# Two transformer blocks on one core: seven block products in place of eight for the feed-forward up projections

## The reference, cut to what matters

```python
D_MODEL, SEQ, D_FF = 1024, 512, 2816

def _swiglu(h, w13, w2):
    g, u = jnp.split(h @ w13, 2, axis=-1)
    return (jax.nn.silu(g) * u) @ w2

def _sublayer(x, fn, pre_g, post_g, shift, scale, gate, res_w):
    h = _rmsnorm(x, pre_g) * (1.0 + scale[:, None, :]) + shift[:, None, :]
    y = _rmsnorm(fn(h), post_g)
    return x + res_w * (1.0 + gate[:, None, :]) * y
...
        mod = (c_act @ ada_w[l] + ada_b[l]).reshape(bsz, N_SUB, 3, D_MODEL)
```

## Time and profile before

| | us |
|---|---|
| median of 3 runs | 3217.52 |
| lowest and highest | 3217.0, 3223.48 |
| span of the profiled execution | 3213.7 |

### The profile page before, as it was taken

How to read it: one execution, slowest core, us unless ns; L and a number is a source line. 1 busy time by engine, 2 the same in 40 slices (tenths; PEclk the granted TensorE clock), 3 DMA queues, 4 the chain that set the end, 5 groups by cost and what they waited for, 6 DMA issues and landing times. The chain is left out here.

```text
span 3213.7 us, 52487 instructions
## 1 busy us (share of the span) xinstructions
PE 3045.3 (95%) x20065; PEld 2461.7 (77%) x20065; DVE 1728.6 (54%) x3224; ACT 1155.9 (36%) x2075; POOL 1349.1 (42%) x893
## 2 busy tenths in 40 slices
PE   5999999899999999999999999999888889999998
PEld 4888876678887888877788887987666667778887
DVE  6445478654445566232666114537677754674443
ACT  3222235432223322234332223226544434435343
POOL 3444443244444434453434444224767660143332
PEclk8999999999999999999999999999999999999999
DMA  7655432155544554332255334213222233222222
GB/s 216 195 184 173 158 85 73 53 170 183 183 156 153 167 180 135 97 90 79 86 163 151 94 93 136 79 53 112 65 58 58 56 107 73 91 77 71 82 66 59
DMA packets 641381, 366.02 MB, mean 114 GB/s; under 512 B 107902, under 2 KB 634132, under 8 KB 640688
## 3 DMA queue, kind: packets, MB, share of 16 engines
q1 hardware_dynamic: 633216, 351.57, 37.2%
q10 hardware_dynamic: 6640, 10.49, 1.1%
q0 software_dynamic: 1344, 1.44, 0.2%
HBM read 334.27 MB, written 24.97 MB: 112 GB/s over the span
## 5 line engine op out<-in xcount | busy, mean ns | idle before, releaser
L270 POOL TENSOR_TENSOR w_lo<-w_raw,w_hi 128x1024 fp32r<-128x1024 f32 (+1 forms) x333 | 786.6, 2362 | 1316.6 <-ACT w_hi L262 1263.9
L335 PE MATMUL acc<-h,w_hi 128*128 128x512 f32 x2256 | 704.4, 393 | 0.0
L262 ACT ACTIVATE w_hi<-w_raw 128x1024 fp32r<-128x1024 f32 (+1 forms) x332 | 344.6, 1038 | 941.1 <-PE acc L335 687.9
L335 PEld LDWEIGHTS acc<-h,w_hi 128*128 128x128 f32 x2256 | 417.3, 188 | 84.6 <-issue 1.8
L335 PE MATMUL acc<-h,w_lo 128*128 128x512 f32 x1128 | 440.3, 390 | 0.0
L335 PE MATMUL acc<-hid,w_hi 128*128 128x512 f32 x1056 | 326.3, 390 | 0.0
L716 DVE SCALAR_TENSOR_TENSOR ada_part<-ada_raw,c_act,ada_part 128x256 f32<-128x256 f32 x672 | 315.0, 489 | 18.6
L335 PEld LDWEIGHTS acc<-h,w_lo 128*128 128x128 f32 x1128 | 211.7, 188 | 45.8
L335 PEld LDWEIGHTS acc<-hid,w_hi 128*128 128x128 f32 x1056 | 197.3, 188 | 40.7
L335 PE MATMUL spare<-h,w_hi 128*128 128x512 f32 x688 | 211.7, 389 | 0.0
L335 PE MATMUL acc<-hid,w_lo 128*128 128x512 f32 x528 | 205.6, 389 | 0.0
(11 more groups left out here) (700 smaller groups left out, 6094.7 us busy)
## 6 DMA issues: line engine op xcount, KB each, us to landing
w_raw<-in_ffn_w SPq DMA_DIRECT2D x240, 512.0 KB, 4.0
ada_raw<-in_ada_w SPq DMA_DIRECT2D x88, 1024.0 KB, 5.0
w_raw<-in_od_w_in SPq DMA_DIRECT2D x32, 512.0 KB, 4.0
w_raw<-in_ffn_w SPq DMA_DIRECT2D x32, 384.0 KB, 3.1
w_raw<-in_ev_w_in SPq DMA_DIRECT2D x22, 512.0 KB, 3.9
image<-inverse_wait SPq DMA_DIRECT2D x144, 64.0 KB, 2.1
first_ada<-in_ada_w SPq DMA_DIRECT2D x8, 1024.0 KB, 12.4
w_raw<-in_ab_w_in SPq DMA_DIRECT2D x16, 512.0 KB, 4.0
```

Source lines behind the costliest of these rows:

```text
L262: act.activation(K.w_hi[:, first % SPLIT, 0:tiles, :], K.raw[:, first % RAW, 0:tiles, :], ACT.Copy).then_inc(K.hi_ready, 1)
L270: pool.tensor_tensor(K.w_lo[:, first % SPLIT, 0:tiles, :], K.raw[:, first % RAW, 0:tiles, :], K.w_hi[:, first % SPLIT, 0:tiles, :].bitcast ...
L335: mm = pe.matmul(out, w[:, slot, k, :], moving(ap, k, tokens), start=first and k == 0 and p == 0, stop=last and k == tiles - 1 and p == le ...
```

## The change

With Strassen's scheme (in Winograd's form) a product of 2 by 2 blocks takes seven block products in place of eight, and some additions of blocks. The blocks here are halves of the 1024 features (4 tiles each), the two chunks of a turn (gate and up), and halves of the 512 tokens (256 columns each). So:

- Turns 0 to 2 of each phase stay as they are (without modulation pieces). Turns 3 to 21 are made of seven products of 4 tiles by 3 passes with 256 columns: 84 in place of 48 products of TensorE.
- Four sums of blocks of `h` are made once a phase, on VectorE, then split: high part on ScalarE, low part on VectorE (128 by 1024 elements each). For them the entry keeps the full `h` too (`h_full`): ScalarE writes each block twice, and `low` reads the full block and the high part, both from SBUF.
- Per turn VectorE makes four sums of weights: one operation of 1024 elements and two of 512, all from SBUF to SBUF. GpSimd makes the low parts in five pieces, two of 1024 and three of 512 elements (2 of 1024 before); ScalarE the high parts likewise.
- The seven results in PSUM are combined by VectorE in four operations a turn (three of 512 elements and one of 256), with one copy of 256 on ScalarE; silu now reads SBUF.
- The high and low parts of the hidden values are no longer made in each turn but all at the end: 22 high parts on ScalarE, 17 low parts on VectorE, 5 on GpSimd, while the first down turn runs.
- Pieces of modulation are spread anew: one vector's eight sums a turn at most, in three portions between the other operations. Phases 0 and 2 have one a turn in turns 3 to 21, and 7 and 8 in down turns; phase 3 has one in turns 3 to 13, the two vectors of four pieces in turns 14 to 21, and 8 pieces of two vectors in its down turns; phase 5 four pieces in turns 3 to 10 and 8 in its down turns.

The core of the diff (blank lines left out):

```diff
+        if full is not None:
+            act.activation(full[:, b, :], S.tp[b % 2][:], ACT.Identity, bias=shift[:, b:b + 1]).then_inc(S.h_full, 1)
...
+        if full is not None:
+            dve.wait_ge(S.h_full, b + 1)
+            dve.tensor_tensor(S.h[:, LO, b, :], full[:, b, :], S.h[:, HI, b, :].bitcast(F32), ALU.subtract).then_inc(S.h_ready, 1)
+            return
...
+PLAIN = 3
+HALF = SEQ // 2
+KH = DB // 2
+HI_PLACE = {1: 1, 7: 2, 6: 3, 3: 4, 4: 5}
+LO_PLACE = {5: 1, 7: 1, 1: 2, 2: 2, 6: 3, 3: 4, 4: 5}
+ADA_UP = {0: {t: (t - 3, None) for t in range(3, FB)},
+          2: {t: (t + 23, None) for t in range(3, FB)},
+          3: {**{t: (t + 50, None) for t in range(3, 14)}, **{t: (64 + (t - 14) // 2, t % 2) for t in range(14, FB)}},
+          5: {t: (76 + (t - 3) // 2, (t - 3) % 2) for t in range(3, 11)}}
+ADA_DOWN = {0: range(19, 26), 2: range(45, 53), 3: range(68, 76), 5: range(80, 88)}
...
+        moving = {1: h[:, :, 0:KH, 0:HALF], 2: h[:, :, KH:DB, 0:HALF], 3: h[:, :, KH:DB, HALF:SEQ],
+                  5: t_of[0], 6: t_of[1], 7: t_of[2], 4: t_of[3]}
...
+                for t in range(PLAIN + 2, FB):
+                    n = base + 2 * t
+                    sp.wait_ge(S.lo, 5 * (t - PLAIN - 1))
+                    chunk_load(n + 1, up.sources[1](t))
+                    sp.wait_ge(S.left_done, t - PLAIN - 1)
+                    chunk_load(n, up.sources[0](t))
+                    ada_until(t)
...
+                def lo(t, p):
+                    tau = t - PLAIN
+                    pool.wait_ge(S.hi, 5 * tau + HI_PLACE[p])
+                    if p == 7:
+                        pool.wait_ge(S.sums, 3 * tau + 2)
+                    elif p in (1, 6):
+                        pool.wait_ge(S.sums, 3 * tau + 3)
+                    if p in (1, 7):
+                        out, full, top = both_lo(t, p), both_full(t, p), both_hi(t, p)
+                    else:
+                        out, full, top = lo_of(t, p), full_of(t, p), hi_of(t, p)
+                    pool.tensor_tensor(out, full, top.bitcast(F32), ALU.subtract).then_inc(S.lo, 1)
...
+                for j in range(2):
+                    split_lo(pool, K, up, 2, 2, j, 8)
+                for t in turns:
+                    for p in (7, 1, 6, 3, 4):
+                        lo(t, p)
+                pool.sem_inc(K.lo_ready, 2 * count)
+                for j in range(2):
+                    split_lo(pool, K, down, 0, 0, j, tiles[j])
+                for j in range(8, 13):
+                    pool.wait_ge(S.hid_hi, j + 1)
+                    pool.tensor_tensor(hid[:, j, :], hid_full[:, j, :], hid_hi(j).bitcast(F32),
+                                       ALU.subtract).then_inc(S.hid_pool, 1)
...
+                quick_pre_act(act, K, S, base, shift, update, full=h_full)
+                plain(0)
+                for j in range(2):
+                    split_hi(act, K, up, 2, 2, j, 8)
+                hi(PLAIN, 1)
+                term_hi(1, 2)
+                hi(PLAIN, 7)
+                hi(PLAIN, 6)
+                plain(1)
+                term_hi(2, 3)
+                term_hi(0, 3)
+                hi(PLAIN, 3)
+                hi(PLAIN, 4)
+                term_hi(3, 4)
+                plain(2)
+                for t in turns:
+                    if t + 1 < FB:
+                        hi(t + 1, 1)
+                    else:
+                        act.sem_inc(K.hi_ready, 2 * count)
+                        down_hi(0)
+                    copy_first(t)
+                    if t > PLAIN:
+                        silu(t - 1)
+                    if t + 1 < FB:
+                        for p in (7, 6, 3, 4):
+                            hi(t + 1, p)
+                    else:
+                        down_hi(1)
+                hidden_hi(0, 16)
+                silu(FB - 1)
+                split_hi(act, K, down, 0, 0, 2, tiles[2])
+                hidden_hi(16, FB)
...
+                def product(t, p):
+                    pe.wait_ge(S.lo, 5 * (t - PLAIN) + LO_PLACE[p])
+                    for k in range(KH):
+                        for part in (HI, LO):
+                            pe.matmul(out_of[p], hi_of(t, p)[:, k, :], moving[p][:, part, k, :], start=k == 0 and part == HI, stop=False)
+                    for k in range(KH):
+                        mm = pe.matmul(out_of[p], lo_of(t, p)[:, k, :], moving[p][:, HI, k, :], start=False, stop=k == KH - 1)
+                    if p in done:
+                        mm.then_inc(done[p], 1)
...
+                    if tau == 0:
+                        pe.wait_ge(S.prod_ready, 2)
+                        pe.wait_ge(S.h_full, DB)
+                        pe.wait_ge(S.t_ready, 4)
+                    else:
+                        pe.wait_ge(S.left, tau)
+                    product(t, 1)
+                    product(t, 2)
+                    if pending is not None:
+                        ada_pe(pe, K, FIRST_ADA + pending, K.ada_of(pending)[0].vecs, K.ada_acc, S.ada_cols)
+                    q, v = ADA_UP[index].get(t, (None, None))
+                    pending = None if v == 0 else q
+                    product(t, 6)
+                    if tau:
+                        pe.wait_ge(S.u_second, tau)
+                    product(t, 5)
+                    product(t, 7)
+                    if tau:
+                        pe.wait_ge(S.outer, tau)
+                    product(t, 3)
+                    product(t, 4)
...
+                def sums_first(t):
+                    tau = t - PLAIN
+                    slots_free(dve, t)
+                    chunk_landed(dve, t, 0)
+                    chunk_landed(dve, t, 1)
+                    q = (base + 2 * t) % RAW
+                    quarters = K.raw[:, q:q + 2].rearrange("p c (a k) w -> p (c a) (k w)", a=2)
+                    both = (K.w_sums[:, 0].rearrange("p (a k) c -> p a (k c)", a=2), K.z[:, 4:6, :])[t % 2]
+                    dve.tensor_tensor(both, quarters[:, 2:3].broadcast_to([P, 2, KH * P]), quarters[:, 0:4:3],
+                                      ALU.subtract).then_inc(S.sums, 1)
+                    dve.wait_ge(S.sums, 3 * tau + 1)
+                    dve.tensor_tensor(sum_full(t, 6), full_of(t, 1), sum_full(t, 5),
+                                      ALU.subtract).then_inc(S.sums, 1)
+                def sums_second(t):
+                    tau = t - PLAIN
+                    dve.wait_ge(S.sums, 3 * tau + 2)
+                    dve.tensor_tensor(sum_full(t, 3), full_of(t, 2), sum_full(t, 6),
+                                      ALU.subtract).then_inc(S.sums, 1)
+                def combine_left(t):
+                    tau = t - PLAIN
+                    dve.wait_ge(S.left_done, tau + 1)
+                    dve.wait_ge(S.copied, tau + 1)
+                    if tau:
+                        dve.wait_ge(S.sil, tau)
+                    dve.tensor_tensor(left, pairs[0], p1_copy.broadcast_to([P, 2, HALF]), ALU.add).then_inc(S.left, 1)
+                def combine_right(t):
+                    tau = t - PLAIN
+                    dve.wait_ge(S.right_done, tau + 1)
+                    dve.wait_ge(S.left, tau + 1)
+                    dve.tensor_tensor(right, pairs[1], left[:, 1:2].broadcast_to([P, 2, HALF]), ALU.add).then_inc(S.right, 1)
+                    dve.wait_ge(S.right, tau + 1)
+                    dve.tensor_tensor(u_rows[:, 1], right[:, 1], out_of[5], ALU.add).then_inc(S.u_second, 1)
+                def combine_outer(t):
+                    dve.wait_ge(S.turn_done, t - PLAIN + 1)
+                    dve.wait_ge(S.u_second, t - PLAIN + 1)
+                    dve.tensor_tensor(right, right, pairs[2], ALU.add).then_inc(S.outer, 1)
+                def gated(t):
+                    dve.wait_ge(S.sil, t - PLAIN + 1)
+                    row = hid_full[:, t, :].rearrange("p (a c) -> p a c", a=2)
+                    dve.tensor_tensor(row, row, u_rows, ALU.mult).then_inc(S.prod_ready, 1)
...
+                quick_pre_dve(dve, K, S, shift, update, h_full)
+                dve.wait_ge(S.h_full, DB)
+                b11, b12 = h_full[:, 0:KH, 0:HALF], h_full[:, 0:KH, HALF:SEQ]
+                b21, b22 = h_full[:, KH:DB, 0:HALF], h_full[:, KH:DB, HALF:SEQ]
+                whole = [t[:, LO] for t in t_full]
+                term(1, whole[0], b12, b11, ALU.subtract)
+                term(2, whole[1], b22, whole[0], ALU.add)
+                plain(0)
+                sums_first(PLAIN)
+                sums_second(PLAIN)
+                term(3, whole[2], b12, b22, ALU.add)
+                term(4, whole[3], b21, whole[1], ALU.subtract)
+                term_lo(1, 1)
+                plain(1)
+                term_lo(2, 2)
+                term_lo(0, 3)
+                term_lo(3, 4)
+                plain(2)
+                pending = None
+                for t in turns:
+                    q, v = ADA_UP[index].get(t, (None, None))
+                    vec = v or 0
```

(28 more changed lines are left out.)

369 lines of the change are left out of this document (255 added, 114 removed).

## The result

| | before | after |
|---|---|---|
| median, us | 3217.3 (3217.0 to 3223.5) | 3357.3 (3353.0 to 3357.9) |
| span of the profiled execution | 3213.7 | 3350.7 |

A forecast was written before the change was run, and what follows sets the result against it. The prediction took TensorE, busy 95% of the span, as the bound, and port waits as the new turns' bound. Its terms, -50 - 4 + 17 + 21 + 21 + 5 + 21 = +31 us on 3217.5, gave 3249; range 3205 to 3285.

The forecast's parts named there:

- Products: Strassen turns on TensorE: 256-column products at 0.1198 us, 10.53 us a turn with a piece, saving 0.8 in each of 76.
- The port: SBUF port shared by VectorE and GpSimd: waits make a loop of 11.05 us a turn, longer than TensorE's 10.53.
- So they take turns: VectorE's SBUF sums and GpSimd's splits alternate at the port; two GpSimd operations lose 0.43 us each.
- Turns 3 to 21: Strassen turns in four phases: five at 10.5 us, then 14 at 11.05; 878 us become 828, -50.
- Entry: Entry blocks: the low part waits for GpSimd's addition, 0.95 us later for each of six blocks in three phases; +21 us.
- Start of turn 3: Before turn 3: port work outlasts TensorE's cover by about 5.3 us; +21 for four phases, +5 for the clock.
- End: First down turn: low parts alternate between VectorE and GpSimd, 1.72 us a pair; 5.7 us, 4 in phase 5; +21.
- Pieces in down turns: Modulation pieces moved into down turns lengthen those by 0.93 us each, with a last piece in the first; +17 us.
- Their sums hide beside 15 us of products: Down turns: VectorE's sums for the moved pieces add no time beside TensorE's products.
- (2): Rival, faster: operations do not hold the port, turns run at TensorE's 10.53 and 10.06 us; -50, 3167 us; chance 0.09.
- (3): Rival: one-time costs are small, turn 3 and the end cost a third, 14 us; -2, 3215 us; chance 0.18.
- (4): Rival, slower: TensorE stays at half clock in entry, turn 3's start and end; +34, 3283 us; chance 0.15.

The follow-up runs named there:

- 12: Changed kernel, with GpSimd's low part of the fifth weight piece covering only 8 columns from turn 7 on; 3311.9 us.
- 6: Changed kernel, with the entry's low part reading the scaled input in PSUM again and ScalarE writing the full block behind it; 3346.6 us.
- 7: Changed kernel; before turn 3 GpSimd splits the gate chunk first, the other four pieces only after VectorE's last low part of the terms; 3345.9 us.
- 8: Changed kernel, with all low parts of the hidden tiles on VectorE and GpSimd's five gone; 3356.5 us.
- 13: Kernel 10, with the fifth piece's low part on VectorE instead of GpSimd in every Strassen turn, behind the turn's modulation piece; 3246.4 us.
- 15: Kernel 13, with VectorE taking the fifth low part right behind the combination that ends the turn before; 3215.4 us.
- 16: Kernel 15, with ScalarE making the first of the eight terms of each piece's vector; 3212.9 us.
- 10: Changed kernel with 5, 6 and 7 together, plus all hidden low parts on VectorE, pausing after tile 15 for GpSimd's third-chunk split; 3235.5 us.
- 1: Changed kernel, with ScalarE taking the border operations of the block before ahead of its third split in a down turn; 3283.2 us.
- 5: Changed kernel; border work ahead of the third split, piece's products behind the next down turn's first chunk, left-over piece's products after the first chunk; 3257.4 us.
- 17: Kernel 16, with the fifth low part behind the turn's first two weight sums instead of ahead of them; 3271.3 us.
- 4: Changed kernel, with unneeded products before the piece's products in down turns 1 to 6 of phases 3 and 5; 3340.5 us.

## Why the prediction was wrong, step by step

- **Products:** right; 256 columns in 0.12 us, TensorE's turn 10.52 when nothing holds it (12).
- **The port:** right as what lengthens turns, entry and start (6, 7, 12); "So they take turns" is wrong as a rule (8).
- **Turns 3 to 21:** -50 was mis-sized. 11.24 us in three phases instead of 11.05, and reached after three turns, not five; the low clock took 2.5 us of turn 3 in three phases and 1.6 in phase 5, 9 in all, not 5. I had taken GpSimd's load as the loop; 13, 15 and 16 show a chain across VectorE, ScalarE and GpSimd, and it counted VectorE's 9.4 us as "full as well" where, without waits for the port, 10.52 is possible.
- **Entry:** right, 3.17 us a block for 3.12, and 19 us for 21. I priced it as a loss of its own; 6 shows that a good third of what a shorter entry gives (6 of 15 us) is lost again to the port's queue before turn 3.
- **Start of turn 3:** gap 3.4 to 3.7 for 5.3, and its cause is shown (7). The 5.3 has a slip besides: 20.9 us begun 1.2 late against a cover of 16.4 make 5.7.
- **End:** right, 5.9 us in phases 0 and 2, 5.7 in phase 3 and 4.2 in phase 5, for 5.7 and 4. But taking the steps of 1.69 away gave nothing in 8 and 5 us in 10, where 14 to 20 were expected.
- **Pieces in down turns:** the step that failed. "Their sums hide beside 15 us of products" compared lengths, 7.3 and 3.0 against 15.0, and not starts. VectorE's order puts border work ahead of the sums, ScalarE's order puts the third split ahead of the border work, and the split waits for TensorE. I read that the pieces had been moved and priced their products on TensorE, 0.93 each, which 1 and 5 show to be right to 0.02; I did not follow what stands ahead of them in the queues. I had put their wait at nothing; in the changed kernel TensorE is idle for 67 us before the pieces' products, in 18 waits, and runs at half clock behind them. 5 shows that this step alone is the 100 us.
- **Rivals:** (2) is out, the waits for the port are there in every stage; (3) is out, the start of turn 3 and the end cost 35 us by the landmarks, not 14; (4), half clock in entry and end, did not happen; the clock fell where I had no wait at all.

## What to carry to other kernels

Work moved into another stage costs its own length only if its start fits too: write down for that stage what is ahead of it on its own engine, and what that waits for, back to the engine that will wait in the end. Here a reorder that costs nothing (5: three places in the code, 100 us) was worth more than all the work that TensorE was spared (57 us). And operations that want the same port are best placed where the other engine is idle: in 17 a place that misses by 0.07 us costs 2.3 us a turn.

## What the runs showed that I had not expected

VectorE's operations without a pause keep GpSimd off the port altogether: a split of 128x768 took some 8.3 us beside fourteen of them (8), while in the changed kernel, in the same stage, the two had alternated in steps of 1.69. What decides between the two patterns no run here shows. A GpSimd split over only 8 columns still took 1.20 us in 12, beside a sum of VectorE of 1.35 us:

```profile
869.09 1.20 POOL L1127 TENSOR_TENSOR h<-w_raw,h 128x8 fp32r<-128x8 f32 x1
...
868.88 1.35 DVE L1356 TENSOR_TENSOR w_sums<-w_raw 128x1024 f32<-128x1024 f32 x1
```

My prediction weighed the rule of the Trainium skill, SBUF — State Buffer, Who interferes with whom, of a lock held for a whole instruction. The rows of 12 and 17 agree with it: the wait of a short operation is as long as what remains of the other's, 2.3 us for 0.6 of work in 17. The rows of 8 show that the one that waits does not always come next. And idle for 3.0 us was enough for TensorE to return at half clock (a product of 512 columns in 0.43 us, not 0.23), which cost 1.6 to 1.8 us each time (4).
